# High and low weights of three rotating SBUF places stored side by side, with the raw weights in a place of their own

## What is computed

```
for l in (0, 1):
    hn = rmsnorm(x, norm_mix_pre[l])
    if l == 0: m = mixer_even(hn)          # hn @ w_in (1024 x 2048), gating, recurrence, @ w_out (1024 x 1024)
    else:      m = mixer_odd(hn)           # hn @ w_in (1024 x 3072), short convolution, @ w_out (1024 x 1024)
    x = x + rmsnorm(m, norm_mix_post[l])
    hn = rmsnorm(x, norm_ffn_pre[l])
    f = square(relu(hn @ mlp_up[l])) @ mlp_down[l]     # 1024 x 4096 and 4096 x 1024
    x = x + rmsnorm(f, norm_ffn_post[l])
```

## Time and profile before

| what | value |
|---|---|
| median of three runs | 2157.94 us |
| span of the profiled execution | 2155.1 us |
| time of a run less the profiled span | 2.8 us |
| TensorE matmul, busy | 2146.0 us, 13496 matmuls |
| TensorE weight load, busy | 2135.0 us, 13496 loads |
| VectorE, busy | 908.0 us |
| ScalarE, busy | 652.9 us |
| GpSimd, busy | 100.1 us |

### The profile page before, as it was taken

The page is one execution under the profiler, slowest core; times in us unless marked ns, Lnnn a source line. Parts: engine busy times, 40 slices in busy tenths (PEclk is TensorE's granted clock), DMA queues, the critical chain, the costliest instruction groups (busy, mean ns, idle before and its releaser), DMA issues.

```text
span 2155.1 us, 31488 instructions
## 1 busy us (share of the span) xinstructions
PE 2146.0 (100%) x13496; PEld 2135.0 (99%) x13496; DVE 908.0 (42%) x1414; ACT 652.9 (30%) x1105; POOL 100.1 (5%) x127
## 2 busy tenths in 40 slices
PE   9999999999999999999999999999999999999998
PEld 9999999999999999999999999999999999999998
DVE  8766367323322322334953333493223223322336
ACT  6673355202301310333511112453013103202332
POOL 2000000000000000000043231000000000000000
PEclk9999999999999999999999999999999999999999
DMA  5111422111111111141311114222111111111142
GB/s 165 35 41 40 139 88 72 50 40 49 50 42 47 49 50 40 49 135 44 120 50 47 43 50 139 67 84 59 42 48 50 49 40 50 50 42 48 50 140 81
DMA packets 208410, 138.65 MB, mean 64 GB/s; under 512 B 6000, under 2 KB 204784, under 8 KB 208272
## 3 DMA queue, kind: packets, MB, share of 16 engines
q1 hardware_dynamic: 207552, 135.51, 20.6%
q10 hardware_dynamic: 720, 1.13, 0.1%
HBM read 119.22 MB, written 17.40 MB: 63 GB/s over the span
## 4 chain that ended last, share of the span: by engine, by line
PE 99%; ACT 1%; DMA 0%; DVE 0%; issue 0%; DVEq 0%; ACTq 0%
PE ps L698 32%; PE ps L700 32%; PE ps L699 32%; PE ps L773 1%; PE ps L801 0%; PE ps L729 0%; PE ps L720 0%; DMA w_all_raw<-in_w_in_even_dram 0%; PE ps L716 0%; PE ps L784 0%; PE ps L760 0%; ACT L1074 0%; ACT L1030 0%; ACT lru L1030 0%; ACT lru L1032 0%; ACT gelu L1074 0%
## 5 line engine op out<-in xcount | busy, mean ns | idle before, releaser
L698 PE MATMUL ps<-x_hi,w_all 128*128 128x352 f32 x2304 | 747.0, 324 | 0.0
L700 PE MATMUL ps<-x_hi,w_all 128*128 128x352 f32 x2304 | 739.1, 321 | 0.0
L699 PE MATMUL ps<-x_lo,w_all 128*128 128x352 f32 x2304 | 739.1, 321 | 0.0
L698 PE MATMUL ps<-h_hi,w_all 128*128 128x352 f32 x1728 | 556.2, 322 | 0.0
L700 PE MATMUL ps<-h_hi,w_all 128*128 128x352 f32 x1728 | 555.2, 321 | 0.0
L699 PE MATMUL ps<-h_lo,w_all 128*128 128x352 f32 x1728 | 555.2, 321 | 0.0
L698 PEld LDWEIGHTS ps<-x_hi,w_all 128*128 128x128 f32 x2304 | 432.4, 188 | 2.7
L699 PEld LDWEIGHTS ps<-x_lo,w_all 128*128 128x128 f32 x2304 | 432.4, 188 | 2.2
L700 PEld LDWEIGHTS ps<-x_hi,w_all 128*128 128x128 f32 x2304 | 432.3, 188 | 0.0
L876 ACT CAST w_all<-w_all_raw 128x1024 fp32r<-128x1024 f32 x166 | 173.5, 1045 | 525.1 <-DMA w_all_raw<-in_mlp_down_dram 324.8
L698 PEld LDWEIGHTS ps<-h_hi,w_all 128*128 128x128 f32 x1728 | 324.5, 188 | 0.3 <-DVE h_lo L1452 0.3
(11 more groups left out here) (201 smaller groups left out, 1416.0 us busy)
## 6 DMA issues: line engine op xcount, KB each, us to landing
w_all_raw<-in_mlp_up_dram SPq DMA_DIRECT2D x60, 512.0 KB, 3.9
w_all_raw<-in_mlp_down_dram SPq DMA_DIRECT2D x60, 512.0 KB, 3.8
x_save<-f SPq DMA_DIRECT2D x9, 1408.0 KB, 6.0
x_old<-x_save SPq DMA_DIRECT2D x9, 1408.0 KB, 11.5
w_all_raw<-in_c_w_in_dram SPq DMA_DIRECT2D x22, 512.0 KB, 3.7
w_all_raw<-in_w_in_even_dram SPq DMA_DIRECT2D x12, 512.0 KB, 3.6
x_old<-in_x_cols_dram SPq DMA_DIRECT2D x3, 1408.0 KB, 12.8
w_all_raw<-in_w_out_even_dram SPq DMA_DIRECT2D x6, 512.0 KB, 3.8
```

Of the source, the lines that this page charges most:

```text
L698: nc.tensor.matmul(dst, wh, hi, start=(i == 0), stop=False)
L699: nc.tensor.matmul(dst, wh, lo, start=False, stop=False)
L700: last = nc.tensor.matmul(dst, wl, hi, start=False, stop=(i == KC - 1))
```

## The change

In the rotating places, each high weight now lies next to its low weight: high, low, high, low, and so on. A block of 128 high weights is read with a step of 8 bytes over 1024 bytes, and the 128 low weights with the same step from 4 bytes further on. ScalarE now reads `w_raw` and writes with a step of 8 bytes; VectorE reads `w_raw` and the high weights with a step of 8 bytes, and writes the low weights with a step of 8 bytes. The places `s`, `x`, `ha` and `hb` and all activations stay as they are, and so do the orders of all engines and all waits.

```
+W_SHIFT = (0, 4, 24)
+WS = len(ROTATING) * 2 * D + 32
...
-        w_all = place("w_all", [P, 6, D], F32R)
-        w_all_raw = place("w_all_raw", [P, 6, D], F32, at_w)
+        w_all = place("w_all", [P, WS], F32R)
+        w_raw = place("w_raw", [P, len(ROTATING), D], F32)
...
                 s = ROTATING.index(slot)
-                three = [w[:, i, :].rearrange("p (k n) -> p k n", k=KC)
-                         for w, i in ((w_all, 2 * s), (w_all, 2 * s + 1), (w_all_raw, 2 * s + 1))]
+                at = s * 2 * D + W_SHIFT[s]
+                pairs = w_all[:, at:at + 2 * D].rearrange("p (k n two) -> p two k n", two=2, n=P)
+                three = [pairs[:, 0], pairs[:, 1], w_raw[:, s, :].rearrange("p (k n) -> p k n", k=KC)]
...
-    nc = _bacc.Bacc("TRN2", target_bir_lowering=False, num_devices=1)
+    nc = _bacc.Bacc("TRN2", target_bir_lowering=False, num_devices=1, dynamic_dma_scratch_size=2048)
```

## The result

The changed kernel takes 2185.27 us (median of four runs, 2185.09 to 2185.43), the kernel before 2158.03 us beside it: a ratio of 1.0126, 95% interval 1.0111 to 1.014. The change costs 27 us where 90 us of gain were forecast.

What follows compares the result with a forecast made beforehand. TensorE's own stream was taken as the bound, busy 2146.0 of 2155.1 us. 2155.1 - 96 + 1 + 5 = 2065.1 us of span, plus 2.8, gave 2068 us; range 2020 to 2115, or to 2310 with both slower rivals.

Steps and rivals of the forecast that it cites:

- the count of 12168 matmuls: TensorE's matmuls that read rotating weights: 169 panels x 72 = 12168, each expected to gain.
- the cover of the rounding and the subtraction: On ScalarE and VectorE: even doubled they stay hidden, with 12.9 us of cover against 2.3 us more.
- the one from equal paces to a gain: In TensorE's rotating weight reads: a faster read brings matmuls near 151 ns apart, units to 3.62 us; forecast's chance 0.54.
- the explanations that expect no change: Rival for TensorE's matmul stream: the kernel's time stays the same; chance 0.12.
- the two slower rivals: For TensorE's weight reads: doubled toll, chance 0.24, and standing meeting, chance 0.10; range with both up to 2310 us.
- gain 7.9 x 12168 = -96 us: In TensorE's matmuls with rotating weights: 7.9 ns gained on each of 12168, -96 us in all.
- Point (d): On TensorE: weight loads themselves are not stretched, 186 to 192 ns under fast matmuls, 186 to 190 at the gates.
- The price of the steps: 8-byte steps in rounding (ScalarE) and subtraction (VectorE): unchanged, or doubled by +174 and +202 us, hidden even then.
- the +1 us for the first 60 us: At the start, where cover is thin: some six half-size pieces, at most 4 us if doubled; price taken +1 us.
- Raw place 0 us: Loads of raw weights to their new place: same loads, waits, bytes and queue, so 0 us.
- scratch 0 us: The smaller scratch costs nothing, as SP or ScalarE issues all loads and GpSimd none.
- What a faster TensorE runs into: VectorE and ScalarE chains from 60 to 200 us and norm chains at three stage starts: 5 us given back, bounds 0 and 25.

Runs made afterwards that it cites:

- run 3: The kernel before with 256 instead of 352 moving columns in 23 of a unit's 24 matmuls, rest of the product left out: 1716.06 us.
- run 4: The kernel before with weight loads of 64 instead of 128 values in 22 of a unit's 24 matmuls: 2162.21 us.
- run 16: The kernel before with 320 moving columns in 23 of 24 matmuls: 2011.96 us.
- run 2: The changed kernel with no shift at any rotating place, W_SHIFT = (0, 0, 0): 2173.45 us, ratio 1.0072.
- run 13: The changed kernel with no shifts and without the 128 free bytes behind the weights: 2173.62 us, ratio 1.0072.
- run 14: The changed kernel, shifts kept, with 256 instead of 128 free bytes behind the weights: 2185.07 us, ratio 1.0125.
- run 10: The changed kernel with weight loads of 64 values in 22 of 24 matmuls: 2168.59 us.
- run 8: The changed kernel without shifts, p0 and p1 sharing one stretch with four values side by side (step of 16 bytes), p2 in pairs: 2768.99 us, ratio 1.283.
- run 9: The kernel before with raw weights apart and the small scratch, high and low weights in rows, no free bytes behind the weights: 2157.95 us, ratio 1.0001.
- run 5: The kernel before with only the smaller scratch for dynamic DMAs: 2158.5 us, ratio 1.0001.
- run 1: The changed kernel with high and low weights in rows of their own again, raw weights apart, 128 free bytes behind the weights: 2176.98 us, ratio 1.0087.
- run 12: The changed kernel with 256 moving columns in 23 of 24 matmuls: 1723.74 us.

## Why the prediction was wrong

**The reading of the bound was right.** TensorE's own stream sets the time: the distances from unit to unit, added up from the fifth unit to the last, have grown by 28.2 us, of the 28.5 us of the span, while TensorE's waits for other engines add up to 1.9 us before and 1.6 us after. The pace of 158.33 and 160.0 ns and the count of 12168 matmuls held, and so did the cover of the rounding and the subtraction, which TensorE never waits for in the changed kernel.

**The step that failed is the one from equal paces to a gain.** The author took a part of every spacing for a loss of the moving read, which gives way to the weight read where both want the same part of the memory, and took a weight read at nearly the moving read's pace to be free of it (1024 bytes in the 108 ns of the earlier trace rows, 9.5 bytes per ns, beside 8.9). No trace shows such a meeting, nor how long the columns alone take; both were the author's estimate, and so is the gain of 7.9 ns a matmul: no run shows this term. What the runs showed in its place is 27.2 us / 12168 = 2.2 ns more, and no median of a place with moving x below 158.33 ns. The support was the float32 gate matmul, 296 ns a pass for 353 columns, with transposes of 128 columns at 108 ns: 0.836 ns a column and 1 ns left at none, so that the slower moving read seemed to pay next to nothing. But a column that takes twice the 0.413 ns of run 3 changes many things at once, and runs 3, 4 and 16 changed one each: 96 columns less, 64 weights less, 32 columns less. The spacing changed by -39.6, by +1.2 with moving x, and by -11.7 ns; an estimated 13 ns of it go neither with the columns nor with the weights. Run 2 is the plain test of equal paces: without shifts, all three places ran at 160.0 ns, not near 151. The reads may still meet once for each load at a fixed price; equal paces don't free them from it. Of the explanations that expect no change, a price by the number of weights falls with run 4, and something in the issue of loads is left, unproven. None of the rivals has the measured time. That the measured 2185 us lies inside 2020 to 2310 is no merit: the range reached there only for the two slower rivals, which did not happen.

**The term "gain 7.9 x 12168 = -96 us" measured +27 us**: +15 for the layout side by side at any place (runs 2 and 13), from 158.33 to 160.0 ns, nothing where 160.0 stood already, and +12 for the shifts (after against run 2, run 14): 8.5 at p2, 1.1 in the middle h strip of p1, and 0.8 in p0's first h strip, whose own layout is that of run 2 but which often follows a unit of p2. The two slower rivals, a weight read that costs twice as much at all places and two reads that stay together at one place, are refuted by sizes that small: p0 and p1 rose by 1.7 ns and p2 by 4.1, and the upper end of their range, 2310 us, lies 125 us above the time measured.

The float32 reading itself stands, and what it means is open. A float32 pass of 353 columns takes 296 ns and a float32 transpose of 128 columns 108 ns, with a load of 128 weights beneath each: 1 ns is left at no columns, by the same estimate that leaves 13 for fp32r. So the 13 ns are a price of the fp32r matmuls of this stream, not of every matmul and not of every load. Whether the slower pace or the number format makes the difference, no run separates. The transposes' 108 ns may thus be nothing but the pace of their own columns (128 x 0.836 = 107), and bound the weight read only from above; run 4's 0.84 ns a weight, 107.5 ns for 128, happens to agree.

**Point (d) held for contiguous loads and failed for the step**: the loads lasted 194 instead of 188 ns, by 0.047 ns a weight (run 10). The longer loads don't set the pace, though: the spacing doesn't follow the load until run 8. Run 8 showed with a step of 16 bytes that three engines slow down (a load from 188 to 330 ns, a rounding from 1045 to 2042, a subtraction from 1216 to 2022); that the 6 ns at 8 bytes are the small end of the same effect is the author's guess, not shown. The price of the steps, taken as nothing after the first 60 us, was 82 ns apiece on ScalarE and 3 ns (by the medians) on VectorE, and hidden, as reckoned; of the +1 us for the first 60 us, at most 0.3 us came (the first loads of line 701 start at 22.8 us, those of line 698 at 22.5). "Raw place 0 us" and "scratch 0 us" held (runs 9 and 5), though where the raw weights and what follows them lie modulo 256 can matter (run 1). "What a faster TensorE runs into" was never put to the test.

**What stays open**: how the load's extra 6 ns become 1.67 ns or 4 ns of spacing, if they do at all. It isn't proportional to the load (run 10), nor to the cover (run 12). A load starts with one matmul and serves the next (before, line 699's load and line 698's matmul both start at 518.90 us, line 699's matmul at 519.06), so at 188 ns it is recorded to end some 30 ns after its own matmul's start, and at the 134 ns of run 4 some 25 ns ahead of it, at nearly the same spacing. Most units stand at 158.33, 160.0, 162.5, 163.3 or 166.7 ns, others between; a whole unit repeats them to 0.01 us, some stretches hold one and drop it only at a break (run 1), and a unit can carry on its forerunner's. That hints at a stream that settles into one of several rhythms, chosen by addresses and by the last break. What sets those rhythms, and what the 13 ns are, no run here shows. Moving the middle h strip by 128 bytes, which might bring its 160.0 ns to 158.33 (an estimate: 1728 x 1.67 = 2.9 us), wasn't tried.

## What to carry to other kernels

When a part of the spacing of matmuls is put down to memory reads that collide, change the columns and the weights one at a time first: runs 3 and 4, each with a part of the work left out, would have spoken against it beforehand. Keep the stationary operand contiguous: side by side with a step of 8 bytes cost 0.7%, and a step of 16 bytes at two of three places 28%. After any change of layout in such a stream, read the spacing unit by unit: 128 free bytes behind the weights cost 0.9% in one layout and nothing in another, and a comparison that lets such places move blames the wrong edit. And where a mean grows, look at the median too: seven long subtractions of 166 made the mean here.

## What the runs showed of the hardware that was not expected

- The same matmuls with the same addresses of both operands ran at 158.3 ns or at 166.7 ns for stretches of 60 to 252 us, depending on 128 free bytes behind the weights, which move the raw weights and the small tensors (runs 1 and 9).
- In the layout of the kernel before, fp32r matmuls with 128 weights start 158.3, 146.6 and 118.7 ns apart with 352, 320 and 256 columns (before, runs 16 and 3), and 159.5 with 64 weights and 352 columns (run 4): 0.413 ns a column between 352 and 256, and by estimate some 13 ns that go with neither. A float32 pass of 353 columns takes 296 ns and a float32 transpose of 128 columns 108: 0.836 ns a column, and 1 ns left at none.
- With a step of 16 bytes a load of 128 weights lasts 330 ns instead of 188, and matmuls start 233.3 ns apart; an element takes 2.0 instead of 1.0 ns on ScalarE (median 2042 instead of 1045 ns for 1024) and 2.0 instead of 1.2 on VectorE (2022 instead of 1216 ns). With 8 bytes VectorE's median is the old one but for 3 ns (1219 instead of 1216).
- Where a subtraction on VectorE and a product on GpSimd start within 0.1 us of each other, the one that starts second takes about 0.8 to 1.0 us longer: GpSimd's 1.95 instead of 0.95 us before the change, VectorE's 2.02 instead of 1.22 us after it (seven pairs in each trace; GpSimd's product starts 63 to 81 ns behind the subtraction before the change, 0 to 24 ns ahead of it after).
